# Two norms of a hybrid encoder block, each worked through in halves of the tokens

## The reference

```python
def rmsnorm(x, g):
    xf = x.astype(jnp.float32)
    y = xf * lax.rsqrt(jnp.mean(xf * xf, axis=-1, keepdims=True) + EPS)
    return (y * g.astype(jnp.float32)).astype(x.dtype)

def swiglu(x, w_in, w_out):
    gate, up = jnp.split(x @ w_in, 2, axis=-1)
    return (jax.nn.silu(gate) * up) @ w_out

h = rmsnorm(x, ffn1_pre_norm)
x = x + 0.5 * rmsnorm(swiglu(h, w_ffn1_in, w_ffn1_out), ffn1_post_norm)
h = rmsnorm(x, mix_pre_norm)
y = hybrid_mixer(h, w_in, ...)
x = x + rmsnorm(y, mix_post_norm)
h = rmsnorm(x, ffn2_pre_norm)
x = x + 0.5 * rmsnorm(swiglu(h, w_ffn2_in, w_ffn2_out), ffn2_post_norm)
```

## Time and profile before

| | |
|---|---|
| median of 3 runs | 1489.06 us |
| the profiled execution | 1489.92 us |
| its span, first to last instruction | 1488.1 us |
| mean granted TensorE clock | 0.998 |
| TensorE busy | 1477.8 us (99%) |
| VectorE, ScalarE busy | 722.7 us (49%), 586.4 us (39%) |
| read from memory | 134.00 MB, 91 GB/s over the span |

### The profile page before, as it was taken

How to read it: one execution, slowest core, us unless ns; L and a number is a source line. 1 busy time by engine, 2 the same in 40 slices (tenths; PEclk the granted TensorE clock), 3 DMA queues, 4 the chain that set the end, 5 groups by cost and what they waited for, 6 DMA issues and landing times.

```text
span 1488.1 us, 20133 instructions
## 1 busy us (share of the span) xinstructions
PE 1477.8 (99%) x7516; PEld 1221.5 (82%) x7516; DVE 722.7 (49%) x1153; ACT 586.4 (39%) x940; POOL 20.1 (1%) x35
## 2 busy tenths in 40 slices
PE   9999999999999999999999999999999999999998
PEld 7888888887898888888888888888878888888886
DVE  6444444223763455454246665654347444444223
ACT  5233233223432555553254654553344332233122
POOL 0000000000100000000000000000000000000000
PEclk9999999999999999999999999999999999999999
DMA  5322223332332222222322222223331222322332
GB/s 192 99 96 90 96 99 99 99 97 89 120 102 91 88 72 89 71 60 97 99 86 71 71 72 70 72 68 99 100 116 68 87 97 99 98 89 95 100 99 99
DMA packets 39397, 137.68 MB, mean 93 GB/s; under 512 B 4743, under 2 KB 4743, under 8 KB 39344
## 3 DMA queue, kind: packets, MB, share of 16 engines
q1 hardware_dynamic: 37728, 132.14, 27.4%
q0 software_dynamic: 1472, 4.76, 1.2%
q10 hardware_dynamic: 144, 0.04, 0.0%
HBM read 134.00 MB, written 2.13 MB: 91 GB/s over the span
## 4 chain that ended last, share of the span: by engine, by line
PE 96%; DVE 1%; ACT 1%; DMA 1%; issue 0%; SPq 0%; DVEq 0%; ACTq 0%
PE ps L290 27%; PE ps L291 27%; PE ps L292 27%; PE ps L872 1%; PE ps L874 1%; PE ps L873 1%; PE ps L1158 1%; PE ps L1138 1%; PE ps L1037 1%; PE ps L1038 1%; PE ps L1036 1%; PE ps L1518 1%; PE ps L1535 1%; PE ps L1123 1%; PE ps L1541 1%; PE ps L1505 1%
## 5 line engine op out<-in xcount | busy, mean ns | idle before, releaser
L269 ACT ACTIVATE whi<-raw 128x1024 fp32r<-128x1024 f32 x238 | 251.9, 1059 | 615.4 <-PE ps L292 553.9
L290 PE MATMUL ps<-hh,whi 128*128 128x512 f32 x1248 | 492.0, 394 | 1.8 <-DVE hl L748 1.0
L291 PE MATMUL ps<-hl,whi 128*128 128x512 f32 x1248 | 486.2, 390 | 0.0
L292 PE MATMUL ps<-hh,wlo 128*128 128x512 f32 x1248 | 485.9, 389 | 0.0
L274 DVE TENSOR_TENSOR wlo<-raw,whi 128x1024 fp32r<-128x1024 f32 x238 | 291.5, 1225 | 394.5 <-ACT whi L269 394.2
L290 PEld LDWEIGHTS ps<-hh,whi 128*128 128x128 f32 x1248 | 234.2, 188 | 55.8 <-issue 2.9
L292 PEld LDWEIGHTS ps<-hh,wlo 128*128 128x128 f32 x1248 | 234.3, 188 | 49.5
L291 PEld LDWEIGHTS ps<-hl,whi 128*128 128x128 f32 x1248 | 234.4, 188 | 46.9 <-issue 0.2
L451 DVE TENSOR_TENSOR tmp<-ps,rstd 128x512 f32<-128x512 f32 x44 | 30.4, 690 | 121.3 <-PE ps L292 121.3
L290 PE MATMUL ps<-whi,ah 128*128 128x512 f32 x176 | 68.5, 389 | 0.0
L292 PE MATMUL ps<-whi,al 128*128 128x512 f32 x176 | 68.5, 389 | 0.0
(11 more groups left out here) (269 smaller groups left out, 1748.3 us busy)
## 6 DMA issues: line engine op xcount, KB each, us to landing
raw<-in_wstream SPq DMA_DIRECT2D x242, 512.0 KB, 3.3
xt<-in_x_t SPq DMA_DIRECT2D x8, 256.0 KB, 5.7
out<-out_tok SPq DMA_DIRECT2D x8, 256.0 KB, 2.0
bias<-vec_dram POOLq DMA_DIRECT2D x8, 192.0 KB, 3.2
raw<-in_wstream SPq DMA_DIRECT2D x4, 256.0 KB, 4.7
bias<-vec_dram POOLq DMA_DIRECT2D x8, 128.0 KB, 3.3
v_mid<-v_tok POOLq DMA_DIRECT2D x2, 384.0 KB, 4.5
cst<-in_consts POOLq DMA_DIRECT2D x1, 640.0 KB, 5.8
```

Of the source, the lines that this page charges most:

```text
L269: nc.scalar.activation(whi[:, s, :], raw[:, s, :], ACT.Copy).then_inc(head_done, 1)
L290: nc.tensor.matmul(out, w, m, start=start, stop=False)
L291: nc.tensor.matmul(out, w, ml, start=False, stop=False)
L292: return nc.tensor.matmul(out, wl, m, start=False, stop=stop)
```

## The change

**Norms by halves.** `TOKENS` are columns 0 to 255 and 256 to 511. The columns 6 and 7 of both output projections are made for the first half of the tokens, then for the second, and the norm of the first half goes on while TensorE makes the second. For `ffn1_out` only their last 8 of 22 products are split so; the first 14 are made whole, copied out and later joined by an addition (`joined`). Squares, sums over partitions (now 256 columns), Ln, Exp, `scaled`, `added`, `gained` all work on 256 columns, first eight tiles of half 0, then eight of half 1. The repeats of L1904 and L1921 and the functions `columns_*`, `scaled_dve`, `added_dve`, `pre3_*` go.

**Consumers.** Group 0 of `v` takes token tiles 0 and 1 over all of `kt`, then 2 and 3; the moving side stays 512 wide. The bias vectors come after it. The first two pairs of the third layer are made with 256 moving columns, half after half, and the pre-norm's sum moves behind the first projection of pair 2. The second sums of the post-norms stand inside the consumers (`kt` 3 of `v`, the fifth step of the third layer). POOL's loads of the biases wait for 16 parts of `xt`.

**Weights.** New buffers `whi_v`, `wlo_v` and `whi_y`, `wlo_y` hold blocks that are split earlier; the stream's order changes to match: two blocks of `v` ahead of the last two of `ffn1_out`, and pair 1 and pair 0 of the third layer between the blocks of `w_out`.

In `w_out_pe`:

```diff
+            for d in range(KT - 2):
+                pe.wait_ge(split_done, 2 * w_out_pair(d) + d % 2 + 1)
+                if d >= 4:
+                    pe.wait_ge(*counted("post2", "left", d - 3))
+                column(d, 0, slice(0, S)).then_inc(block_done, 1)
+            for half in range(2):
+                for d in (KT - 2, KT - 1):
...
+                    column(d, half, TOKENS[half]).then_inc(block_done if half else sem("half_column"), 1)
```

In `w_out_act`:

```diff
+            head_x(act, first, 0)
+            head_x(act, first, 1)
+            for d in range(KT - 2):
...
+                leave(d, 0, slice(0, S))
+                if d < 2:
+                    head(act, first + 1, d, 2 * first + d + 1)
+                    if d == 1:
+                        head_in(act, whi_y, first + 2, 0)
+                        head_in(act, whi_y, first + 2, 1)
+                else:
+                    head(act, first + 3 + (d - 2) // 2, d % 2, 2 * first + d + 1)
```

In `ffn3_in_pe`:

```diff
+            project(pe, first + 2, 0, ps[:, 5, :], hh, hl)
             pe.wait_ge(*counted("pre3", "acc", KT - 1))
             nc.tensor.matmul(ps[:, 4, :], ones[:], y0[:], start=True, stop=True).then_inc(norm_sem("pre", "sum"), 1)
-            project(pe, first + 2, 0, ps[:, 5, :], hh, hl)
             project(pe, first + 2, 1, ps[:, 6, :], hh, hl)
```

In `ffn1_out_act`, after the stage's blocks:

```diff
+            square_half(6, 0)
+            square_half(7, 0)
+            post1_rstd_act(act, 0)
+            for d in range(3):
+                gained_half(d, 0)
+            square_half(6, 1)
+            gained_half(3, 0)
+            head(act, v, 0, 2 * v - 1)
+            gained_half(4, 0)
+            square_half(7, 1)
+            gained_half(5, 0)
+            post1_rstd_act(act, 1)
+            head(act, v, 1, 2 * v)
+            gained_half(6, 0)
+            gained_half(7, 0)
```

In `ffn1_out_dve`, after the stage's blocks:

```diff
+            joined(6, 0)
+            acc_half(6, 0)
+            joined(7, 0)
+            acc_half(7, 0)
+            for half in range(2):
+                for d in range(KT):
+                    scaled(d, half)
+                    if half == 0 and d == 2:
+                        joined(6, 1)
+                    elif half == 0 and d == 4:
+                        acc_half(6, 1)
+                        joined(7, 1)
+                    elif half == 0 and d == 5:
+                        acc_half(7, 1)
+                    if d >= 1:
+                        gained_half(d - 1, half)
+                    if half == 0 and d in (5, 7):
+                        tail(dve, v, d // 2 - 2)
+                    added(d, half)
+                gained_half(KT - 1, half)
```

In `v_pe`, group 0:

```diff
+            for half in range(2):
+                for kt in range(KT):
+                    b, k = divmod(kt, 2)
+                    pe.wait_ge(*counted("pre2", "ready", KT * half + kt + 1))
+                    if half == 0 and kt == 3:
+                        pe.wait_ge(*counted("post1", "acc", KT + 1))
...
+                    for t in (2 * half, 2 * half + 1):
```

In TensorE's program, in the two joints:

```diff
-            for _ in range(12):
-                nc.tensor.matmul(ps[:, 1, :], whi[:, 0, 0:P], whi[:, 0, S:2 * S], start=True, stop=True)
...
-            for _ in range(24):
-                nc.tensor.matmul(ps[:, 7, :], whi_x[:, 0, 0:P], whi_x[:, 0, S:2 * S], start=True, stop=True)
```

More of the change, by code:

```diff
@@ L353, in ffn3_in_pe @@
             first = FIRST["ffn3_in"]
[L354 to L365, removed]
+            plain = [(kt, j) for kt in range(KT) for j in (1, 0)]
@@ new lines, in ffn3_in_pe @@
+            ends = [(kt, j) for kt in range(KT - 2) for j in (1, 0)]
+            ends += [(kt, j) for j in (0, 1) for kt in (KT - 2, KT - 1)]
+            for half, order in enumerate((plain, ends)):
+                cols = TOKENS[half]
+                for i, (kt, j) in enumerate(order):
+                    pe.wait_ge(*counted("pre3", "ready", KT * half + kt + 1))
+                    if half == 0 and i == 4:
+                        pe.wait_ge(*counted("post2", "acc", KT + 1))
+                        nc.tensor.matmul(ps[:, 6, TOKENS[1]], ones[:], y0[:, TOKENS[1]], start=True, stop=True
+                                         ).then_inc(norm_sem("post2", "sum"), 1)
+                    for s in range(2):
+                        if half == 0 and kt == 0:
+                            pe.wait_ge(split_done, 2 * (first - 1 - 2 * j) + s + 1)
+                        high, low = ((whi_y, wlo_y), (whi_x, wlo_x))[j]
+                        tile = slice(kt * P, kt * P + P)
+                        last = product(ps[:, 2 * j + s, cols], high[:, s, tile], low[:, s, tile], hh[:, kt, cols],
+                                       hl[:, kt, cols], kt == 0, kt == KT - 1)
+                        if half == 1 and kt == KT - 1:
+                            last.then_inc(block_done, 1)
@@ L489, in ffn_in_dve, with y_bank @@
                 turn(j, (0, 1))
[L492 to L508, removed]
+        def y_bank(d):
+            return 4 + d % 4
@@ L509, in columns_pe, with out_bank, ffn1_out_pe @@
+        SPLIT_K = FT - KT
+        OUT_TILES = [(d, k) for d in range(KT - 2) for k in range(FT)]
+        OUT_TILES += [(d, k) for d in (KT - 2, KT - 1) for k in range(SPLIT_K)]
+        OUT_END = {m: d for m, (d, k) in enumerate(OUT_TILES) if k == (FT if d < KT - 2 else SPLIT_K) - 1}
+        def out_bank(d, half):
+            return d - 6 + 2 * half
+        def ffn1_out_pe(pe):
+            first = FIRST["ffn1_out"]
+            for m, (d, k) in enumerate(OUT_TILES):
                 b, i = divmod(m, KT)
@@ L529, in y_bank @@
[L529 to L540 removed]
+            for half in range(2):
+                for d in (KT - 2, KT - 1):
+                    if half == 0:
+                        pe.wait_ge(split_done, 2 * FIRST["v"] + d - 5)
+                    for i in range(KT):
+                        if half == 1 and d == KT - 2 and i == 4:
+                            pe.wait_ge(*counted("post1", "acc", KT - 1))
+                            nc.tensor.matmul(ps[:, 4, TOKENS[0]], ones[:], y0[:, TOKENS[0]], start=True, stop=True
+                                             ).then_inc(norm_sem("post1", "sum"), 1)
+                        k = SPLIT_K + i
+                        last = product(ps[:, out_bank(d, half), TOKENS[half]], *wcols(d % 2, i * P), ah[:, k, TOKENS[half]],
+                                       al[:, k, TOKENS[half]], i == 0, i == KT - 1)
+                    last.then_inc(block_done if half else sem("half_column"), 1)
@@ L857, in v_pe @@
+            bias_vectors_pe(pe)
+            for g in range(1, N_GROUPS):
                 for b in range(4):
@@ L1934, in _ @@
             act.wait_ge(sem("half_set"), 1)
-            columns_act(act, "ffn1_out", "post1", FT, POST1)
+            ffn1_out_act(act)
             v_act(act)
```

487 lines of the change are left out of this document (329 added, 158 removed).

## The result

The changed kernel took 1497.45 us, the median of five executions (1495.39 to 1498.86), beside 1489.29 for the kernel before in the same job: a ratio of 1.0055 with the interval [1.0044, 1.0066]. It is slower by 8.2 us, beyond the 3 us that can be told from no change. The predicted 1496.8 us and its sign were right. The profiled execution took 1497.57 us with a span of 1495.8 us, 7.7 us more than the span of 1488.1 of the kernel before.

The account below looks back on a forecast made before the run. TensorE, busy 1477.8 of 1488.1 us, was taken as the bound. The profiled 1489.92 + 3.2 (joint one) + 2.9 (joint two) + 1.7 (clock) gave 1497.7, or 1496.8 us beside the median; range 1490 to 1505.

Parts of the forecast that it names:

- Step 1: Norm operations of half width, VectorE's and ScalarE's loop: 1.40 us per half tile, 2.80 per tile instead of 2.15.
- Step 2: Half-width matmuls in ffn1_out, w_out and third layer: 0.120 us each, bounds 0.113 and 0.19.
- rival (3): Weight load shows, 0.15 to 0.19 us per half matmul: 1504.5 to 1518 us with the clock; chance 0.08.
- Step 3: Joint one (end of ffn1_out, start of v): rstd 4.7 us earlier, stretch to last hl 7.7 longer; 3.2 us slower.
- (a): Joint one: second half column's block is split only after block 19 ends; TensorE starts at 3.34, waiting 0.46 us.
- Step 4: Joint two (end of w_out, third layer's start): layer starts 4.0 us earlier, later wait of 3.9; 2.9 us slower.
- (e): Joint two, third layer: 192 half matmuls (23.04 us), a sum (0.43), waits of 0.19, 0.57 and 0.54.
- Step 5: Clock falls once more with joint two's 3.9 us gap: 1.7 us added, bounds 0 and 3.4.
- Rival (1): No fall of the clock, all else as predicted: 1495.1 us; chance 0.20.
- Rival (2): Half norms hide: 1480.3 us, if half tiles take under 1.36 and third norm's sum keeps 10 us cover; chance 0.10.
- Rival (4): Gain and loss cancel, one joint's norm hiding or only the order changing: 1486 to 1492 us; chance 0.07.

Follow-up runs that it names:

- e7: Changed kernel with VectorE's addition to xt in joint one done on 8 of 256 columns per half tile: 1492.3 us, ratio 1.0021.
- e6: Changed kernel with three moves in joint one: v bank copies ahead of sums, splits of group 1's next and group 0's last block earlier: 1492.49 us, ratio 1.0026.
- h_joint2: Joint two as in the changed kernel, joint one as in the kernel before: 1494.93 us, ratio 1.0038.
- e4: Changed kernel with VectorE's two copies of v banks 2 and 3 put ahead of four sums of squares: 1493.9 us, ratio 1.0037.
- e5: Changed kernel with both blocks of the third layer's pair 3 rounded and split earlier: 1490.96 us, ratio 1.0012.
- e9: Changed kernel with all five moves, both early splits of pair 3 and the three in joint one: 1488.1 us, ratio 0.9991.
- e2: Changed kernel with the third norm's sum put back ahead of both projections of pair 2: 1498.4 us, ratio 1.0058.
- e3: Changed kernel with pair 3's first block rounded ahead of the third norm's Ln and split ahead of the first product: 1492.58 us, ratio 1.0025.
- h_joint1: Joint one as in the changed kernel, joint two as in the kernel before: 1491.31 us, ratio 1.0016.
- e1: Changed kernel with 15 unneeded 512-column matmuls filling TensorE's 3.58 us gap before the third layer's fourth pair: 1493.31 us, ratio 1.0040.
- e8: h_joint2 with both blocks of the third layer's pair 3 rounded and split earlier: 1488.25 us, ratio 0.9998.

## Why the prediction was right

**Step 1** held: 1.40 us for half a tile. **Step 2** held: 0.120 us for a half matmul, so rival (3) is out; the 0.113 and the 0.19 were the bounds. The Trainium skill's figure for it (TensorE: Matmul & The Clock Gate, Back-to-back issue gap), 0.109 us, is 9% short here.

**Step 3**, joint one, was the right mechanism and 0.4 us too dear: 2.8 measured for 3.2. The first scaled tile came 9.54 us after the zero (9.6), the last `hl` at 36.9 (37.4), and the waits were 0.25, 0.77, 1.43, 0.18 and 1.70 for the predicted 0.46, 1.2, 1.9, 0.5 and 2.1. Each is a little short. In the first, the terms that (a) names add up to 3.09 and not 3.34, and the wait came out 0.21 shorter. e7 and e6 show the two sides of the cause: with a faster loop the order does no harm (3.6 us back), and with a better order the same loop loses next to nothing (2.5 us back).

**Step 4**, joint two, was 0.9 us too dear: 2.0 for 2.9. The order of events and the 47.4 us to the third layer (47.75) were right, and so was the cause of the gap (3.58 for 3.9). The excess is spread over three terms. The block waits in `w_out` were 0.91, 0.43 and 0.60 for 1.2, 1.0 and 0.95, so the third layer began 0.4 sooner; (e), its half matmuls, took 24.4 us for 24.8, with one listed wait of 0.18 and 0.8 us in pauses that the view names no releaser for, in place of waits of 0.19, 0.57 and 0.54; and the gap was 0.3 shorter.

**Step 5**, the clock, was the step that was mis-sized: + 1.7 predicted, 2.9 in the profiled execution. There was one additional fall, as said, but it lasted 6.8 us and not the 3.4 of the earlier trace rows. This made up for what steps 3 and 4 had too much, 1.3 us: that the sum is closer than its terms is luck. And the fall was no certainty: with the same gap of 3.58 us the profiled executions of the changed kernel, h_joint2 and e7 show a fall, those of e4 and e6 none. The Trainium skill's rule on bursts after a wait (TensorE: Matmul & The Clock Gate, HAM oscillation), by which I had called the 1.7 certain, holds here in three of these five traces.

Rival (1), no fall, 1495.1: the two shortest of the five executions, 1495.39 and 1495.98, have a mean clock of 0.998 instead of 0.996 to 0.997. So it describes some executions, not the median. Rival (2) named two conditions, and the runs show both at work: e7 meets the first (1.14 us for a half tile), and e5 makes the second unneeded, as its split no longer stands behind the sum. It promised 1480.3; even with both sets of moves, e9 reaches 1488.1. It left out the waits inside `w_out` (2.1 us in e9) and before the sum (0.77), and VectorE's pace in joint one; how the rest of the 7.8 us divides was not worked out. Rival (4), 1486 to 1492, is out by 3 us.

## What to carry to other kernels

Halving a norm's tiles brings its first result earlier and its last one later. Before doing it, set the halved loop (here 1.40 us, against 1.36 for the consumer) beside its consumer, and list what is queued behind its end. When a sum or a split moves, ask for each chain behind it how much TensorE work covers it: here 11.7 us became 6.3 over a chain of 10. And where a gap appears, look first at whether the waited-for operation needs what it stands behind; four moved operations brought back 6.3 of 8.2 us.

## What was not expected of the hardware

Whether the clock falls to 1.2 GHz after a gap is not settled by the gap's length: five profiled gaps of 3.58 us gave one fall of 6.8 us, two of 3.4 and two of none, and the one of 4.09 in e2 gave 6.8. The wait of 1.7 us in joint one was followed by a fall of 3.4 us in four traces (the changed kernel, e2, e3, h_joint1) and by none in two (e1, e5), and the kernel before itself shows one of 3.4 us without a gap. This goes with the scatter of a kernel's times. In e9 four of eleven executions took 1486.64 to 1487.16 us at a mean clock of 0.999 and the other seven 1487.40 to 1488.45 at 0.998; the medians of the two groups are 1.5 us apart, about the 1.7 of one fall. With such steps a difference of 1 to 2 us in medians has to be read in the trace, and a single trace without a fall proves little.

A load of a block in `w_out` took 5.3 us in h_joint2 and 4.7 in e8, the two kernels with joint two alone, where it was 3.2 in the changed kernel, issued in the same order and within 0.5 us of the same time; behind it TensorE waited 2.69 and 2.18 us. Both traces are of the longest execution of their kernel, so whether this belongs to the kernels or to these executions isn't shown. The cause stays open.
